# Fourteen to six plain up blocks in layer 0, and the fourth weight sum on GpSimd

## The reference

```python
def conv_ffn(h, w_up, conv_w, conv_b, w_down):      # D_FF = 2816, w_up is 1024 x 5632
    a, gate = jnp.split(h @ w_up, 2, axis=-1)
    a = lax.conv_general_dilated(a, conv_w[:, None, :], window_strides=(1,), padding=[(CONV_W - 1, 0)],
                                 dimension_numbers=('NWC', 'WIO', 'NWC'), feature_group_count=D_FF) + conv_b
    return (jax.nn.silu(a) * gate) @ w_down

x = x + y                                            # y: the layer's attention
x = x + conv_ffn(rms_norm(x, ffn_norm[i]), ffn_w_up[i], ffn_conv_w[i], ffn_conv_b[i], ffn_w_down[i])
```

## Time and profile before

| | before |
|---|---|
| median of 3 runs | 1111.0 us |
| the profiled execution | 1111.62 us |
| its span | 1109.8 us |
| TensorE matmul busy | 1098.8 us (99%) |
| VectorE busy | 807.0 us (73%) |
| ScalarE busy | 550.2 us (50%) |
| GpSimd busy | 69.0 us (6%) |
| DMA | 171.35 MB, mean 154 GB/s |

### The profile page before, as it was taken

One profiled execution on the slowest core, in us unless ns is written; L12 is line 12 of the kernel. 1 busy time (PEld: TensorE's weight loads), 2 busy tenths in 40 slices (PEclk: granted clock), 3 DMA queues, 4 the chain that ended last, 5 costly groups with the idle time before them and its releaser, 6 DMA issues.

```text
span 1109.8 us, 17573 instructions
## 1 busy us (share of the span) xinstructions
PE 1098.8 (99%) x6408; PEld 984.2 (89%) x6408; DVE 807.0 (73%) x1374; ACT 550.2 (50%) x1064; POOL 69.0 (6%) x116
## 2 busy tenths in 40 slices
PE   9999999999999999999999999999999999999997
PEld 8999888888899988888999999788889999998886
DVE  6888866557998863337788788857998888876335
ACT  6878653222255433335666666645344554443334
POOL 1111101111000000000111111110000000000000
PEclk9999999999999999999999999999999999999999
DMA  6767546999556422226888777777446656422322
GB/s 201 213 184 182 103 153 186 220 169 233 152 153 180 147 76 94 94 94 190 199 161 173 172 171 136 130 191 171 140 127 199 199 171 177 143 95 98 98 102 99
DMA packets 196330, 171.35 MB, mean 154 GB/s; under 512 B 14425, under 2 KB 176438, under 8 KB 196278
## 3 DMA queue, kind: packets, MB, share of 16 engines
q1 hardware_dynamic: 182430, 120.32, 35.9%
q0 software_dynamic: 13824, 50.34, 23.6%
q10 hardware_dynamic: 24, 0.01, 0.0%
HBM read 168.55 MB, written 52.43 MB: 199 GB/s over the span
## 4 chain that ended last, share of the span: by engine, by line
PE 91%; DVE 5%; ACT 2%; issue 1%; DMA 1%; SPq 0%; DVEq 0%; ACTq 0%
PE ps L766 23%; PE ps L767 23%; PE ps L768 23%; PE ps L842 15%; PE ps L883 2%; PE ps L1065 2%; PE ps L1084 1%; PE ps L944 1%; DMA raw<-in_a_w_in 1%; ACT w_hi L1429 1%; DVE w_lo L2012 0%; DVE h_lo L2044 0%; DVE xT L2376 0%; DVE x_tok L2731 0%; DVE ssacc L2037 0%
## 5 line engine op out<-in xcount | busy, mean ns | idle before, releaser
L768 PE MATMUL ps<-h_hi,w_hi 128*128 128x256 f32 (+1 forms) x704 | 233.2, 331 | 0.0
L767 PE MATMUL ps<-h_lo,w_hi 128*128 128x256 f32 (+1 forms) x704 | 233.2, 331 | 0.0
L766 PE MATMUL ps<-h_hi,w_lo 128*128 128x256 f32 (+1 forms) x704 | 233.2, 331 | 0.0
L1429 ACT ACTIVATE w_hi<-raw 128x512 fp32r<-128x512 f32 (+2 forms) x180 | 146.0, 842 | 86.0 <-PE ps L768 83.1
L2012 DVE TENSOR_TENSOR w_lo<-raw,w_hi 128x512 fp32r<-128x512 f32 (+2 forms) x180 | 167.9, 957 | 11.2 <-ACT w_hi L1429 11.0
L766 PEld LDWEIGHTS ps<-h_hi,w_lo 128*128 128x128 f32 x704 | 133.8, 190 | 12.6
L768 PEld LDWEIGHTS ps<-h_hi,w_hi 128*128 128x128 f32 x704 | 133.8, 190 | 12.5
L767 PEld LDWEIGHTS ps<-h_lo,w_hi 128*128 128x128 f32 x704 | 133.8, 190 | 12.4
L842 PE MATMUL ps<-w_hi,h_lo 128*128 128x384 f32 x368 | 126.1, 343 | 0.6 <-DVE w_lo L2012 0.4
L842 PE MATMUL ps<-w_hi,h_hi 128*128 128x384 f32 x368 | 125.7, 342 | 0.0
L842 PE MATMUL ps<-w_lo,h_hi 128*128 128x384 f32 x368 | 125.5, 341 | 0.0
(11 more groups left out here) (254 smaller groups left out, 2229.8 us busy)
## 6 DMA issues: line engine op xcount, KB each, us to landing
w_sums<-in_ffn_w_up POOLq DMA_DIRECT2D x72, 512.0 KB, 7.7
raw<-in_ffn_w_up SPq DMA_DIRECT2D x64, 512.0 KB, 5.2
raw<-in_ffn_w_down SPq DMA_DIRECT2D x44, 512.0 KB, 3.3
raw<-w_sums SPq DMA_DIRECT2D x24, 768.0 KB, 7.0
w_sums<-w_sums POOLq DMA_DIRECT2D x24, 512.0 KB, 7.3
raw<-in_b_w_in SPq DMA_DIRECT2D x24, 512.0 KB, 5.8
raw<-in_ffn_w_up SPq DMA_DIRECT2D x24, 256.0 KB, 3.0
s_raw<-w_sums SPq DMA_DIRECT2D x24, 256.0 KB, 3.7
```

What stands on the lines that cost most here:

```text
L766: pe.matmul(out_, a_lo, b_hi, start=start, stop=False)
L767: pe.matmul(out_, a_hi, b_lo, start=False, stop=False)
L768: return pe.matmul(out_, a_hi, b_hi, start=False, stop=stop)
L1429: act.activation(w_hi[:, s, at], raw[:, s, at], ACT.Copy).then_inc(hi_done, 1)
```

## The change

Layer 0 gets 6 plain blocks instead of 14, and 16 blocks in seven products, as layer 1 has. Its sums become two chunks of 1024 columns, 8 rounds. S4 is no longer made in HBM: the round loses its fourth copy and its last accumulation (`DMAS` 8 to 6, three steps), and S4's DMA into `s4_raw` goes. Instead GpSimd adds two of the quarters that lie in `raw[s]` into `s4_raw` with one tensor_tensor of 128 x 512 (`fourth_sum`), once per seven-product block, after the load of the block has landed and `fourth_low` of the block before is done. ScalarE's `fourth_high` waits for that add, and so does VectorE's second `seven_low` of a block, because its semaphore frees the slot for the next load. Rounds 0 to 5 of layer 0 run one after the other from the landing of `attnA` block 3 on. Rounds 6 and 7 are issued a step at a time between the fourth sums of blocks 6 to 11. In layer 1 the eight rounds start when block 1 of `attnB` has landed.

```diff
-PLAIN = (14, 6)
-CHUNKS = (1, 2)
+PLAIN = (6, 6)
+CHUNKS = (2, 2)
...
-DMAS = 8
-BEFORE_ROUND = {(0, 0): ("attnA", 3), (0, 3): ("up0", 3), (1, 2): ("attnB", 2)}
+DMAS = 6
+ROUNDS = 8
+LATE_ROUNDS = (2, 0)
+BEFORE_ROUND = {(0, 0): ("attnA", 3), (1, 0): ("attnB", 1)}
...
@@ def load(ph, s, turn, wait):
                 elif wait == "before" and ph[:4] == "down":
                     sp.wait_ge(wlo_done, 2 * nth(layer(ph), FB - 2 + s))
+                    sp.wait_ge(s4_done, nth(layer(ph), FB - 2 + s))
...
-            def load_fourth(l, f):
...
@@ def load_seven(l, s, f):
                     sp.wait_ge(wlo_done, nth(l, f) * 2 - 4)
+                    if is_block(f, PLAIN[l] + 2, PLAIN[l] + 3):
+                        sp.wait_ge(s4_done, nth(l, f) - 2)
...
+            def sum_step(l, n, step):
...
+                if step == 0:
+                    if done:
+                        pool.wait_ge(sum_landed, done)
+                    pool.dma_start(s1, part(1, gate)).then_inc(sum_landed, 16)
+                    pool.dma_start(s3, part(0, a)).then_inc(sum_landed, 16)
+                    pool.dma_start(s2, part(0, a)).then_inc(sum_landed, 16)
+                elif step == 1:
+                    pool.wait_ge(sum_landed, done + 3 * 16)
+                    pool.dma_start(s1, part(0, gate), accum_op=ALU.add, max_dma_last_dim=last).then_inc(sum_landed, 16)
+                    pool.dma_start(s3, part(0, gate), accum_op=ALU.add, max_dma_last_dim=last).then_inc(sum_landed, 16)
+                else:
+                    pool.wait_ge(sum_landed, done + 5 * 16)
+                    pool.dma_start(s2, s1, accum_op=ALU.add, max_dma_last_dim=last).then_inc(sum_landed, 16)
+
+            def fourth_sum(l, s, f):
+
+                pool.wait_ge(raw_landed[s], landed(f"up{l}", s, (f - s) // 2) if isinstance(f, int)
+                             else f * 24 + (landed(f"up{l}", s, PLAIN[l] // 2) - 24 * (PLAIN[l] + s)))
+                if l or not is_block(f, PLAIN[l]):
+                    pool.wait_ge(s4lo_done, nth(l, f) - 1)
+                pool.tensor_tensor(s4_raw[:, :], raw[:, s, 5 * QC:6 * QC], raw[:, s, 2 * QC:3 * QC], ALU.add)\
+                    .then_inc(s4_done, 1)
...
+                for n in range(ROUNDS - LATE_ROUNDS[l]):
...
+                    for step in range(3):
+                        sum_step(l, n, step)
+                begun = PLAIN[l]
+                for n in range(ROUNDS - LATE_ROUNDS[l], ROUNDS):
+                    for step in range(3):
+                        fourth_sum(l, begun % 2, begun)
+                        sum_step(l, n, step)
+                        begun += 1
+                while begun % 2 or begun < PLAIN[l] + 2:
+                    fourth_sum(l, begun % 2, begun)
+                    begun += 1
+                with pool.Fori(begun // 2, FB // 2) as r:
+                    for s in range(2):
+                        fourth_sum(l, s, r * 2 + s)
...
@@ def fourth_high(l, f):
-                act.wait_ge(s4_landed, nth(l, f) * 16)
+                act.wait_ge(s4_done, nth(l, f))
...
@@ def seven_low(l, s, f, half):
                 dve.wait_ge(whi_done, nth(l, f) * 2 - (1 - half))
+                if half and not is_block(f, PLAIN[l], PLAIN[l] + 1):
+                    dve.wait_ge(s4_done, nth(l, f))
```

More of the change, by code:

```diff
@@ L231, in trunk @@
             angcos = sb("angcos", [P, NT, HALF], F32, st)
-        w_sums = [nc.dram_tensor(f"w_sums{l}", (4 * HALF_D, (FB - PLAIN[l]) * P), F32) for l in range(2)]
+        w_sums = [nc.dram_tensor(f"w_sums{l}", (3 * HALF_D, (FB - PLAIN[l]) * P), F32) for l in range(2)]
         def quarter(ap):
@@ L632, in load_seven @@
                   .then_inc(raw_landed[s], 16)
-                if is_block(f, PLAIN[l]):
-                    load_fourth(l, f)
-                elif not is_block(f, PLAIN[l] + 1):
-                    load_fourth(l, f - 1)
             def v_at(ph):
@@ L684, in _ @@
                     for c in range(CHUNKS[l]):
-                        for f in range(begun, PLAIN[l] + c * SUM_COLS[l] // P // 2 * 2 + 2):
+                        for f in range(begun, PLAIN[l] + c * SUM_COLS[l] // P // 2 * 2 + (2 if c else 4)):
                             load_seven(l, f % 2, f)
@@ L725, in _ @@
                     pool.memset(tensor[(1 - e) * HD:(2 - e) * HD, e, :].bitcast(F32), 0.0).then_inc(kz_done, 1)
-            def weight_sums(l, rows, c, done):
+            def sum_step(l, n, step):
+                done = (n + l * ROUNDS) * DMAS * 16
+                c, rows = n // HK * SUM_COLS[l], n % HK * P
                 wv, sums = ffn_w_up[l], w_sums[l]
-                a, gate = PLAIN[l] * P + c, PLAIN[l] * P + c + F
+                a, gate, last = PLAIN[l] * P + c, PLAIN[l] * P + c + F, 4 * SUM_COLS[l]
@@ L732, in part @@
                 def part(half, at):
                     return wv[half * HALF_D + rows:half * HALF_D + rows + P, at:at + SUM_COLS[l]]
-                s1, s3, s2, s4 = (sums[q * HALF_D + rows:q * HALF_D + rows + P, c:c + SUM_COLS[l]] for q in range(4))
-                pool.dma_start(s1, part(1, gate)).then_inc(sum_landed, 16)
-                pool.dma_start(s3, part(0, a)).then_inc(sum_landed, 16)
-                pool.dma_start(s2, part(0, a)).then_inc(sum_landed, 16)
-                pool.dma_start(s4, part(1, a)).then_inc(sum_landed, 16)
@@ L740, in weight_sums @@
-                pool.wait_ge(sum_landed, done + 4 * 16)
-                pool.dma_start(s1, part(0, gate), accum_op=ALU.add, max_dma_last_dim=4 * SUM_COLS[l]).then_inc(sum_landed, 16)
-                pool.dma_start(s3, part(0, gate), accum_op=ALU.add, max_dma_last_dim=4 * SUM_COLS[l]).then_inc(sum_landed, 16)
-                pool.wait_ge(sum_landed, done + 6 * 16)
-                pool.dma_start(s2, s1, accum_op=ALU.add, max_dma_last_dim=4 * SUM_COLS[l]).then_inc(sum_landed, 16)
-                pool.wait_ge(sum_landed, done + 7 * 16)
@@ L746, in weight_sums @@
-                pool.dma_start(s4, s2, accum_op=ALU.add, max_dma_last_dim=4 * SUM_COLS[l]).then_inc(sum_landed, 16)
-                pool.wait_ge(sum_landed, done + 8 * 16)
+                s1, s3, s2 = (sums[q * HALF_D + rows:q * HALF_D + rows + P, c:c + SUM_COLS[l]] for q in range(3))
+                if step == 0:
[11 more added lines that the diff above has]
+                    pool.dma_start(s2, s1, accum_op=ALU.add, max_dma_last_dim=last).then_inc(sum_landed, 16)
@@ L749, in after_load @@
             def after_load(ph, i):
                 pool.wait_ge(raw_landed[i % 2], landed(ph, i % 2, i // 2))
-            done = 0
             for l in range(2):
-                rounds = [(c, rows) for c in range(0, (FB - PLAIN[l]) * P, SUM_COLS[l]) for rows in range(0, HALF_D, P)]
-                for n, (c, rows) in enumerate(rounds):
+                for n in range(ROUNDS - LATE_ROUNDS[l]):
                     if (l, n) in BEFORE_ROUND:
                         after_load(*BEFORE_ROUND[l, n])
-                    weight_sums(l, rows, c, done)
-                    done += DMAS * 16
+                    for step in range(3):
+                        sum_step(l, n, step)
```

13 lines of the change are left out of this document (1 added, 12 removed).

## The result

| | before | after |
|---|---|---|
| median of the runs | 1110.9 us (1110.78 to 1111.54, 5 runs) | 1115.54 us (1114.08 to 1118.34, 5 runs) |
| profiled execution / its span | 1111.62 / 1109.8 us | 1114.44 / 1112.7 us |
| TensorE busy | 1098.8 us | 1093.7 us |

The ratio is 1.0043, 95% interval 1.0032 to 1.0054: slower by 0.4%. The forecast was 1105.0 us with a range up to 1111.0; it was wrong in sign.

What follows compares the result with a forecast made beforehand. TensorE was taken to bound the kernel: 1111.62 us profiled, less 6.4 for eight shorter blocks, plus 0.5 for DMA, gives 1105.7; the median runs 0.6 lower, so 1105.0 us was forecast, range 1103.8 to 1111.0.

Steps and rivals of the forecast that it cites:

- Bound: Whole kernel: TensorE, busy 1098.8 of 1109.8 us, sets the time; VectorE is second bound in the seven-product stage.
- the 0.80 us a block: Layer 0: eight blocks go from 10.88 to 10.08 us on TensorE, a gain of 6.4 us.
- The add in steady state: Seven-product blocks: GpSimd's add of about 1.2 us fits in VectorE's 1.32 us idle; cost taken as 0, bounds 0 and 36.6.
- x: Time per block that GpSimd's add, with handovers, adds to VectorE's list: 1.3 us, free up to 1.32.
- (a): Seven-product blocks: VectorE just bound, handovers on both sides make the add cost 1.5 us; loss 4.6 us, 1109.6; chance 0.15.
- (b): All 32 seven-product blocks: add serial with VectorE takes over about 1.6 us; slower, 1119 at 1.8 us; chance 0.14.
- The add ahead of the second block: Once per layer: VectorE's seven_low ends 1.9 us before TensorE wants it, and the add uses part of that; no loss.
- DMA between 212 and 290: Layer 0, seven loads and two rounds need 74 us in 76: just fits; bounds 0 and 6 us, 0.5 taken.
- (c): DMA saturated from 212 to 290, TensorE waits around blocks 9 to 15: up to 6 us, 1110.5; chance 0.15.
- The slack of a load: Seven-product loads: issued at 345.20, used at 367.74 two blocks on, 22.5 us for a landing of about 7.1.
- The second chunk of sums: Layer 0, rounds 6 and 7: last step lands at 287, load 14 due about 288; covered, 11 us with slack.
- Small edits: Rounds 4 and 5 beside the last output-weight load, layer 1's earlier rounds, fewer S4 loads: nothing, or 1 us at most.

Runs made afterwards that it cites:

- e9: Kernel after with eight plain blocks in layer 0, no round between the adds, round 5 held back, each layer's second add later: 1107.79 us.
- e6: Kernel after with ten plain blocks in layer 0, no round between the adds, each layer's second add waiting for that block's low part: 1109.65 us.
- e1: Kernel before's plan of blocks and rounds, with only the fourth sum moved to a GpSimd add: 1115.01 us, ratio 1.0033.
- e11: Kernel after, but in layer 1 alone the add for the second seven-product block waits for that block's low part: 1112.53 us.
- e10: e9 with the fourth sum of each layer's first seven-product block made by two chained DMAs instead of the GpSimd add: 1107.01 us.
- e2: Kernel after with layer 0's last two rounds moving an eighth of their columns, same steps and waits; later blocks read first-chunk sums: 1109.45 us.
- e12: e10 with GpSimd making each fourth sum twice in layer 1, from its third seven-product block on: 1112.89 us.
- e3: Kernel after, but in both layers the add for the second seven-product block waits for that block's low part: 1117.88 us.

## Why the prediction was wrong

- **Bound, and the 0.80 us a block: right.** TensorE's busy time fell by 5.1 us where about 6 was said, and the undisturbed blocks come every 10.08 us. e9 against e6 agrees, though they differ in round 5 as well: two more seven-product blocks gave 1.9 us, 1.6 by this price and 0.3 ahead of layer 0's second block.
- **The add in steady state: right.** x was taken as 1.3, measured 1.03 us, threshold 1.32. Rivals (a) and (b) did not come about: behind the second block, layer 1 and e1 keep to 10.08 us throughout. (By the prediction's own formula (b) would have decided from x = 1.54, not 1.57: the gain in its sum is 5.9 us.)
- **The add ahead of the second block: the first step that failed.** The prediction costed this once per layer as "a margin of 1.9 us, of which x is used up", with the rows of a steady block. Those rows don't hold there: ahead of the second seven-product block VectorE has no gap for 36 us and TensorE already waits 0.3 us for it, and there are two adds in it, not one. TensorE's wait grew to 0.9 us in layer 0 and from 0.3 to 2.3 in layer 1, where with the fall of the clock (1.5 us) it came to 3.5. e1, which has the add and its waits without the new plan of blocks and rounds, is 3.7 us slower than before; e11 takes one add out of one of the two places and is 3.0 us faster; e10 takes out the rest, and the wait is 0.3 again. The slowness of the GpSimd add was the rival that was priced; its place was what mattered.
- **DMA between 212 and 290: mis-sized.** Rival (c) had the mechanism and a bound of 6; 0.5 was taken, 4.3 came in the profiled execution, and e11's shows that it can be more. The sum "74 us of work in 76" was read as room. Landings show what it means: with the share at 1.0 a 768 KB load takes 12.2 us and not 7. e2 removes the bytes and leaves the steps, and the loss is gone.
- **The slack of a load: misread, and this is why (c) was taken so low.** The prediction matched the load issued at 345.20 with the use at 367.74, two blocks on, and had 22.5 us for it; the use is the one at 357.72, a block earlier, and the slack beyond the landing is 4.3 us instead of some 15. With 15 a landing of 12 to 14 us would have been hidden; with 4.3 ScalarE waits five times and TensorE three.
- **The second chunk of sums: right.** No block waited for a late sum. The steps went out at 217.38, 239.13, 251.47, 260.67, 272.23 and 283.95, within 5.3 us of the times worked out.
- **Small edits: within the bound here, beyond it elsewhere.** "Nothing, or 1 us at most" was said; the kernel after's profile has 0.6 us, e2's 4.2. Which round does it is not shown. Round 5 is not needed: e12, where it is held back until these weights have landed, still has ScalarE waiting 2.8 us for them and TensorE 1.0. Round 4's last steps run beside the load in each of these profiles, but in e10 too, which has no wait.
- **The sum.** 1111.62 - 6.4 + 0.5 against 1111.62 - 6.4 + 4.3 + 1.0 + 3.7 + 0.3. The chances gave 0.15 to (c) and 0.14 to (b), each alone; that two losses of different origin could come together, each smaller than the gain, had no case.

The median of the runs lies 1.1 us above the profiled execution, and the kernel after spreads over 4.3 us where before spreads over 0.8. e9 and e10, in which no round runs beside the loads of the seven-product blocks and no wait ahead of the second block is over 1.2 us, spread over 0.9 us. Both the landings and the clock vary: e2's slow profile has its 4.2 us at the start at a clock of 1.0, and e11's has the clock at 0.91 in layer 0. How much each makes of the median was not separated.

## What to carry to other kernels

A margin read in steady state says nothing on the passage into it: before an engine is made to take turns with another, list its gaps from the last block of the old stage to the second block of the new one, and price the edit where there is no gap. The DMA work that was worked out to fill 97% of its stretch (74 of 76 us) was not covered; price loads in such a stretch by landings at a share of 1.0, and move the traffic to where the page's slices show room, even if that costs a few blocks of the gain (two blocks less of seven products, 1.6 us, bought 4.3). Match a load's issue with its first use slot by slot before calling the distance slack. Before a wait goes onto an in-order queue, look at what stands behind it: in layer 0 the same two lines cost 5.4 us where a round's step stood behind them beside heavy traffic (e3 against e11), and cost nothing where none did (e6). A profile shows one execution: when it lies at the edge of its runs, as in e2 and e3, check what it has or lacks before explaining the median by it.
